# Running sums, row broadcasts and gated scores of the first block's two attentions on fp32r operands, with masks in bf16

## The reference, cut to what matters

```
w[i, j] = exp(z[i, j] - sum over k from j to i-1 of softplus(z[i, k]))     for j < i, else 0
```

```
s[i, j] = (q_i . k_j) * 128**-0.5 * exp(u[j] - m[i])     for j <= i, else 0
h[i]    = sum_j s[i, j] v_j / max(|sum_j s[i, j]|, floor[i])
```

## Time and profile before

| | |
|---|---|
| median of 3 executions | 3308.29 us (3307.25 to 3311.25) |
| the profiled execution's own time | 3307.8 us |
| span of its trace | 3306.0 us |
| busy share of the span | PE 95%, PEld 83%, DVE 61%, ACT 38%, POOL 37% |
| first stick-breaking score matmul | at 242.94 us |
| first gated `ml_decay` | at 353.67 us |
| last numerator and denominator done | at 412.3 us |

### The profile page before, as it was taken

How to read it: one execution, slowest core, us unless ns; L and a number is a source line. 1 busy time by engine, 2 the same in 40 slices (tenths; PEclk the granted TensorE clock), 3 DMA queues, 4 the chain that set the end, 5 groups by cost and what they waited for, 6 DMA issues and landing times.

```text
span 3306.0 us, 49756 instructions
## 1 busy us (share of the span) xinstructions
PE 3147.9 (95%) x18745; PEld 2743.0 (83%) x18745; DVE 2018.0 (61%) x3200; ACT 1255.9 (38%) x2157; POOL 1213.6 (37%) x593
## 2 busy tenths in 40 slices
PE   5989989998899999999998999899999999999998
PEld 2765568998888888888887888699999965799998
DVE  4663440999987788788886255466632554466622
ACT  2334242444983333333333233432222444432221
POOL 1420034467224454454553322144434510244432
PEclk8999899999999999999999999799999999999999
DMA  5630023456569999999995211022223210122221
GB/s 226 227 103 0 0 89 95 131 168 198 187 228 334 334 340 339 337 347 343 349 351 197 64 46 39 20 90 89 89 89 96 91 39 1 39 89 89 89 90 64
DMA packets 181098, 507.16 MB, mean 153 GB/s; under 512 B 15840, under 2 KB 73184, under 8 KB 176736
## 3 DMA queue, kind: packets, MB, share of 16 engines
q1 hardware_dynamic: 72000, 262.18, 24.2%
q0 software_dynamic: 36864, 134.23, 11.0%
q10 hardware_dynamic: 72096, 108.93, 9.9%
HBM read 465.43 MB, written 39.85 MB: 153 GB/s over the span
## 4 chain that ended last, share of the span: by engine, by line
PE 86%; ACT 6%; DVE 5%; issue 2%; DMA 1%; ACTq 0%; DVEq 0%
PE ps L1178 22%; PE ps L1129 16%; PE ps L1066 14%; PE ps L1413 8%; PE ps L842 6%; ACT arena L1787 2%; PE ps L1296 2%; PE ps L1243 2%; PE ps L892 1%; PE ps L937 1%; ACT arena L1803 1%; PE ps L1560 1%; DVE arena L2221 1%; PE ps L1308 1%; PE ps L1196 1%
## 5 line engine op out<-in xcount | busy, mean ns | idle before, releaser
L2141 POOL TENSOR_TENSOR w_lo<-ring,w_hi 128x1024 fp32r<-128x1024 f32 x296 | 749.8, 2537 | 1515.9 <-ACT w_hi L738 1515.5
L738 ACT ACTIVATE w_hi<-ring 128x1024 fp32r<-128x1024 f32 x500 | 525.0, 1055 | 796.9 <-PE ps L1129 272.1
L1129 PE MATMUL ps<-w_hi,arena_r 128*128 128x512 f32 x1536 | 426.7, 397 | 4.7 <-DVE arena_r L2575 4.7
L1066 PE MATMUL ps<-h_hi,w_hi 128*128 128x384 f32 x1024 | 355.9, 348 | 5.3 <-issue 5.3
L1178 PE MATMUL ps<-h_hi,w_hi 128*128 128x264 f32 x1712 | 351.6, 287 | 2.0 <-DVE arena L2672 2.0
L1178 PE MATMUL ps<-h_lo,w_hi 128*128 128x264 f32 x1712 | 350.3, 286 | 0.0
L1178 PE MATMUL ps<-h_hi,w_lo 128*128 128x264 f32 x1712 | 349.8, 286 | 0.0
L1066 PE MATMUL ps<-h_lo,w_hi 128*128 128x384 f32 x1024 | 349.2, 341 | 0.0
L1129 PEld LDWEIGHTS ps<-w_hi,arena_r 128*128 128x128 f32 x1536 | 289.1, 189 | 72.3 <-DVE arena_r L2575 5.5
L1066 PE MATMUL ps<-h_hi,w_lo 128*128 128x384 f32 x1024 | 346.8, 339 | 0.0
L2564 DVE TENSOR_TENSOR w_lo<-ring,w_hi 128x1024 fp32r<-128x1024 f32 x188 | 228.4, 1222 | 134.3 <-ACT w_hi L738 132.8
(11 more groups left out here) (337 smaller groups left out, 5702.1 us busy)
## 6 DMA issues: line engine op xcount, KB each, us to landing
ring<-weight_stream SPq DMA_DIRECT2D x500, 512.0 KB, 3.8
gates<-arena ACTq DMA_DIRECT2D x12, 2048.0 KB, 7.1
arena<-gates ACTq DMA_DIRECT2D x32, 768.0 KB, 14.4
arena<-w_modulation ACTq DMA_DIRECT2D x16, 1024.0 KB, 6.2
early_acts<-arena ACTq DMA_DIRECT2D x64, 192.0 KB, 2.8
arena<-early_acts ACTq DMA_DIRECT2D x32, 384.0 KB, 7.7
arena<-w_modulation ACTq DMA_DIRECT2D x4, 2048.0 KB, 24.3
x<-x_t ACTq DMA_DIRECT2D x1, 2048.0 KB, 11.4
```

Of the source, the lines that this page charges most:

```text
L738: act.activation(w_hi[:, s, :], ring[:, s, :], ACT.Copy).then_inc(hi_ready, 1)
L1066: last = pe.matmul(ps[:, bank, 0:ND], w, v, start=c == 0 and p == 0, stop=c == DC - 1 and p == 2)
L1129: last = pe.matmul(ps[:, Y_BANKS[b][half], :], a[u], w[v][:, half * BANK:(half + 1) * BANK], start=first and p == 0, stop=final and p == 2)
L2141: pool.tensor_tensor(w_lo[:, s, :], ring[:, s, :], w_hi[:, s, :], ALU.subtract)\
```

## The change

- `sb_between`: softplus is cut into `sp_hi` (ACT, Copy to fp32r, `sb_high`) and `sp_lo` (DVE, difference in place of `sp_buf`, `sb_low`); each of the ten matmuls becomes two in fp32r, one on each part, with the constants `tri` and `neg_ones` rounded to fp32r (`sums_r`).
- The masks `hidden` and `late` and their identity are bf16 copies; ACT makes them and `sums_r` once, near the start of the kernel.
- `ml_decay`: the row of maxima is kept as two parts in one tile `m_parts` of 36 rows (high part in rows 0 to 3, low part in rows 32 to 35, rows between zero), broadcast by one fp32r matmul per block.
- `ml_scores`: q and k are cut into parts (`conv_high` on ACT, `conv_low` on DVE, one chunk of 512 columns in each of the turns h = 1 to 7 and two in the last), and each block has three fp32r matmuls in place of one in fp32.
- Semaphores are merged (`gains_ready` into `mod_ready`, `row_min` into `row_step`, `ffn_zero` into `pads_zeroed`); the points at which engines wait for them stay.

```
@@ PE
-                    last = pe.matmul(causal(0, s)[:, 0:P], ident, cst("hidden"), start=False, stop=True)
+                    last = pe.matmul(causal(0, s)[:, 0:P], ident_b, hidden_b, start=False, stop=True)
             def sb_between(h):
-                pe.wait_ge(sp_ready, h + 1)
+                pe.wait_ge(sp_split, h + 1)
                 wait(pe, logw_ready, h)
...
-                        last = pe.matmul(out[:, (j - s) * P:], cst("tri") if j == s else cst("neg_ones"),
-                                         sp_buf[:, h % 2, o:o + SEQ - j * P], start=j == s, stop=j == TB - 1)
+                        for k, part in enumerate((sp_hi, sp_lo)):
+                            last = pe.matmul(out[:, (j - s) * P:], sums_r[:, 0 if j == s else 1, :],
+                                             part[:, h % 2, o:o + SEQ - j * P], start=j == s and k == 0,
+                                             stop=j == TB - 1 and k == 1)
...
-                    pe.matmul(out, cst("pick_head", ML_HEADS * P, 4)[:, h * P:(h + 1) * P],
-                              m_pad[1][:, SEQ + s * P:2 * SEQ], start=True, stop=False)
-                    last = pe.matmul(out[:, 0:P], ident, cst("late"), start=False, stop=True)
+                    pe.matmul(out, pick_r[:, h * P:(h + 1) * P], m_parts[:, s * P:SEQ], start=True, stop=False)
+                    last = pe.matmul(out[:, 0:P], ident_b, late_b, start=False, stop=True)
...
                 wait(pe, wqk_ready, h)
+                pe.wait_ge(conv_step, CONV1 * DC + ML_HEADS + h + 1)
                 for s in range(TB):
-                    last = pe.matmul(causal(0, s), conv[4 + h][:, s * P:(s + 1) * P], conv[h][:, s * P:SEQ],
-                                     start=True, stop=True)
+                    q, k = ((conv_hi[:, c, lo:hi], conv_lo[c][:, lo:hi])
+                            for c, lo, hi in ((h, s * P, SEQ), (ML_HEADS + h, s * P, (s + 1) * P)))
+                    for i, (w, v) in enumerate(three(q, k)):
+                        last = pe.matmul(causal(0, s), w, v, start=i == 0, stop=i == 2)
@@ ACT
+            act.wait_ge(const_in, 16)
+            for dst, src in ((ident_b, ident), (hidden_b, cst("hidden")), (late_b, cst("late")),
+                             (sums_r.rearrange("p a b -> p (a b)"), cst("sums", 2 * P))):
+                act.activation(dst, src, ACT.Copy).then_inc(cast_done, 1)
...
+            def sb_high(h):
+                act.wait_ge(sp_ready, h + 1)
+                wait(act, between_ready, h - 1)
+                act.activation(sp_hi[:, h % 2, :], sp_buf[:, h % 2, :], ACT.Copy).then_inc(sp_high, 1)
+            def conv_high(c):
+                act.wait_ge(max_step, MAX_STEPS + 2)
+                act.activation(conv_hi[:, c, :], conv[c], ACT.Copy).then_inc(conv_silu, 1)
             sb_copy(0)
             sb_log(0)
+            sb_high(0)
             sb_copy(1)
             for h in range(SB_HEADS):
                 if h + 1 < SB_HEADS:
                     sb_log(h + 1)
+                    sb_high(h + 1)
                 if h == 0:
...
+                    act.wait_ge(max_step, MAX_STEPS + 1)
+                    act.activation(m_parts[0:4, :], m_pad[1][:, SEQ:], ACT.Copy).then_inc(row_act, 1)
+                    act.activation(pick_r, cst("pick_head", ML_HEADS * P, 36), ACT.Copy).then_inc(cast_done, 1)
                 sb_weights(h)
                 if h + 2 < SB_HEADS:
                     sb_copy(h + 2)
+                if h:
+                    conv_high(h - 1)
+                if h == SB_HEADS - 1:
+                    conv_high(h)
@@ DVE
+            def sb_low(h):
+                dve.wait_ge(sp_high, h + 1)
+                dve.tensor_tensor(sp_lo[:, h % 2, :], sp_buf[:, h % 2, :], sp_hi[:, h % 2, :], ALU.subtract)\
+                    .then_inc(sp_split, 1)
+            def conv_low(c):
+                dve.wait_ge(conv_silu, DC + c + 1)
+                dve.tensor_tensor(conv_lo[c], conv[c], conv_hi[:, c, :], ALU.subtract).then_inc(conv_step, 1)
             sb_nabs(0)
             sb_softplus(0)
+            sb_low(0)
+            dve.tensor_copy(m_parts, cst("pick_head", ML_HEADS * P, 36)).then_inc(max_step, 1)
...
                     sb_softplus(h + 1)
                 sb_logw(h)
+                if h + 1 < SB_HEADS:
+                    sb_low(h + 1)
+                if h == 0:
+                    dve.wait_ge(row_act, 4)
+                    dve.tensor_tensor(m_parts[32:36, :], m_pad[1][:, SEQ:], m_parts[0:4, :], ALU.subtract)\
+                        .then_inc(max_step, 1)
+                if h:
+                    conv_low(h - 1)
+                if h == SB_HEADS - 1:
+                    conv_low(h)
```

More of the change, by code:

```diff
@@ L101 @@
 NCONST = 0
-for _n, _k in [("ident", P), ("ones", P), ("ones64", P), ("tri", P), ("neg_ones", P), ("iota", P),
+for _n, _k in [("ident", P), ("ones", P), ("ones64", P), ("sums", 2 * P), ("iota", P),
                ("late", P), ("hidden", P), ("pick_head", ML_HEADS * P), ("first_half", P), ("lowest", CHUNK)]:
@@ L121 @@
 LOG_SEQ = 9
-ROW_STEPS = LOG_SEQ + 3
+PADS = 5
+ROW_MINS = 2
+ROW_STEPS = ROW_MINS + LOG_SEQ + 3
 MAX_STEPS = LOG_SEQ + 2
@@ L252, in build @@
         w_buf = view(5120, 2, 1280, of=work_w)
+        sp_lo = place("sp_lo", [P, 2, 1280], F32R, at=at_w + 2560)
+        sb_r = place("sb_r", [P, 3584], F32R, at=at_h)
+        sp_hi = view(0, 2, 1280, of=sb_r)
+        m_parts = view(2560, SEQ, rows=36, of=sb_r)
+        pick_r = view(3072, ML_HEADS * P, rows=36, of=sb_r)
+        cast = place("cast", [P, 3, P], BF16, at=at_arena + 25200)
+        ident_b, hidden_b, late_b = (cast[:, k, :] for k in range(3))
+        sums_r = view(25392, 2, P, dt=F32R)
+        conv_hi = view(16472, DC, SEQ, dt=F32R)
+        conv_lo = [view(23656, SEQ, dt=F32R)] + [view(6208 + c * (SEQ + CONV1 - 1), SEQ, dt=F32R) for c in range(DC - 1)]
         conv = [view(23656, SEQ)] + [conv_in[:, c, 0:SEQ] for c in range(DC - 1)]
@@ L422, in build @@
         sp_ready = sem("sp_ready")
+        sp_high, sp_split = sem("sp_high"), sem("sp_split")
+        cast_done = sem("cast_done")
         between_ready = sem("between_ready")
@@ L496, in build @@
         zeroed = sem("zeroed")
-        ffn_zero = sem("ffn_zero")
         a_taken = sem("a_taken")
@@ L950, in sb_out @@
                 last.then_inc(y_ready, 1)
+            pe.wait_ge(cast_done, 4)
             sb_scores(0)
@@ L980, in _ @@
             pe.wait_ge(logw_ready, SB_HEADS)
-            pe.wait_ge(conv_silu, 8)
+            pe.wait_ge(cast_done, 5)
+            pe.wait_ge(row_act, 4)
+            pe.wait_ge(max_step, MAX_STEPS + 2)
             def ml_decay(h):
@@ L2245, in _ @@
             dve.memset(conv_in[:, :, 0:CONV1 - 1], 0.0).then_inc(pads_zeroed, 1)
-            dve.wait_ge(pads_zeroed, 5)
+            dve.wait_ge(pads_zeroed, PADS)
             dve.wait_ge(gates_taken, 2)
-            dve.tensor_scalar(n_row, f_row, 0.0, 2.0, ALU.min, ALU.mult).then_inc(row_min, 1)
-            dve.wait_ge(row_min, 1)
-            dve.tensor_tensor(e_row, n_row, f_row, ALU.subtract).then_inc(row_min, 1)
+            dve.tensor_scalar(n_row, f_row, 0.0, 2.0, ALU.min, ALU.mult).then_inc(row_step, 1)
+            dve.wait_ge(row_step, 1)
+            dve.tensor_tensor(e_row, n_row, f_row, ALU.subtract).then_inc(row_step, 1)
             def qk_normed(g):
@@ L2273, in _ @@
             modulation(2 * DC, 4 * DC).then_inc(mod_ready, 1)
-            dve.wait_ge(mod_ready, 2)
+            dve.wait_ge(mod_ready, 3)
             modulated_gain(1, "g_norm2")
@@ L2277, in _ @@
             dve.tensor_scalar(f_row, f_row, 0.0, None, ALU.min).then_inc(row_step, 1)
-            dve.wait_ge(row_step, 1)
+            dve.wait_ge(row_step, ROW_MINS + 1)
             dve.tensor_tensor(f_pad[0][:, SEQ:], f_row, e_row, ALU.subtract).then_inc(row_step, 1)
             for k in range(LOG_SEQ):
-                dve.wait_ge(row_step, k + 2)
+                dve.wait_ge(row_step, ROW_MINS + k + 2)
                 src, dst = f_pad[k % 2], f_pad[(k + 1) % 2]
@@ L2383, in _ @@
             dve.wait_ge(out_added, DC)
-            dve.wait_ge(gains_ready, 2)
+            dve.wait_ge(mod_ready, 4)
             split_normed(dve, s_in2, lambda c: xf[:, c, :], lambda c: gains[:, 1, c:c + 1],
@@ L2792, in ffn @@
                 dve.wait_ge(rstd_ready, n.rooted)
-                dve.memset(a_pad[:, :, 0:CONV2 - 1], 0.0).then_inc(ffn_zero, 1)
-                dve.wait_ge(ffn_zero, k + 1)
+                dve.memset(a_pad[:, :, 0:CONV2 - 1], 0.0).then_inc(pads_zeroed, 1)
+                dve.wait_ge(pads_zeroed, PADS + k + 1)
                 def up(i):
@@ L3058 @@
     constant("ones64", (i // 64 == j // 64).astype(f32))
-    constant("tri", -(i >= j).astype(f32))
-    constant("neg_ones", -np.ones((P, P), f32))
+    constant("sums", np.concatenate([-(i >= j).astype(f32), -np.ones((P, P), f32)], 1))
     constant("iota", j.astype(f32))
@@ L3063 @@
```

(3 more changed lines are left out.)

11 lines of the change are left out of this document (5 added, 6 removed).

## The result

The changed kernel took 3284.32 us (median of 5, 3278.32 to 3290.66) beside 3310.09 us for the kernel before (median of 5, 3307.25 to 3322.22): ratio 0.9915, 95% interval 0.989 to 0.9941. The difference of the medians is 25.8 us; the two profiled spans, 3276.5 and 3306.0 us, differ by 29.5.

A forecast was written before the change was run, and what follows sets the result against it. PE, busy 95% of the span, was taken as the bound until ACT and DVE bind. Terms saved 37.4 us, less 7 for the clock, net 30.4: 3307.8 - 30.4 = 3277.4 us, range 3263 to 3297.

The forecast's parts named there:

- the clock: Allowance for PE running below 2.4 GHz: 7 us, 4 in stick-breaking heads and 3 in gated ones, bounds 0 and 19.
- fill: From 242.94 us to the first head's running sums: 22.7 us against 24.62 before, saving 1.9.
- six turns: Stick-breaking turns, 267.56 to 341.83 us: 10.8 us each, 64.8 against 74.3, saving 9.5.
- start of the gated heads: From 353.67 to 380.67 us: 13.9 us against 27.0 before, saving 13.1.
- Prices: PE step times: 128-column fp32r matmul 0.21 us, bf16 mask 0.15 instead of 0.42; running sums 3.56 against 4.53.
- Half the missing share is lost time: Reading of PEclk before the change: about 9 us lost in stick-breaking heads, about 10 us in gated heads.
- loop of ACT and DVE: In stick-breaking turns, the hand-offs between ACT and DVE take 10.4 us, level with PE's 10.43.
- The forecast's own sign of being wrong: A stick-breaking turn of over 12 us, or any stage after 412 us longer than before.
- rival 3: PE's clock falls in the stick-breaking turns, slower than before: 3323 us at 0.7 throughout, gated heads included; chance 0.04.
- Decay: Gated heads: 36-row fp32r matmul per block and four masks take 1.34 us against 4.50.
- Scores: Gated heads: scores in three passes take 2.2 us against 2.16, no gain, bounds 1.8 and 2.8.
- At no cost: Four casts at the start, under 1.5 us on ACT, and three 0.6 us operations at h = 0 hide in waits.

The follow-up runs named there:

- zero rows: Changed kernel with its four floor-row broadcasts as fp32 matmuls of 128 rows, 124 of them zeros: ratio 0.9898, span 3269.5 us.
- fillers: Changed kernel with 128-row zero-padded broadcasts plus matmuls nobody reads where TensorE waits: ratio 0.9886, span 3267.3 us; with 4-row broadcasts instead, ratio 0.9908.
- the gated heads alone: Kernel before with only decay by parts and gated scores in three passes; masks and running sums as before: ratio 0.9948, span 3289.9 us.
- sums alone: Kernel before with only the running sums in two fp32r passes; masks, decay and gated scores as before: ratio 0.9968, span 3294.6 us.
- masks alone: Kernel before with only the masks in bf16; running sums, decay rows and gated scores as before: ratio 0.9933, span 3290.9 us.
- the last version: Changed kernel with 128-row zero-padded broadcasts, nine unread matmuls ahead of the last running sums, conv_low moved behind the next nabs: median 3272.22 us, ratio 0.9876.
- the full rows: Changed kernel with its four 4-row broadcasts replaced by fp32 matmuls of 128 rows of other data: ratio 0.9892, span 3274.9 us.
- 36 rows and the late take: Changed kernel with floor broadcasts by parts in 36 rows and sb_take moved on DVE behind the low part: ratio 0.9908, span 3278.5 us.

## Why the prediction was right, and where it was not

The forecast of 3277 us in 3263 to 3297 held: 3284.32 measured, and for the profiled execution 29.5 us less span against 30.4 forecast. The sum at full clock was right: the terms without the clock are 131.9 us, and the same stages, measured with the clock held wherever a run shows that, are 132.4. Over these the changed kernel lost 8.0 us to the clock, where 7.0 had been set aside. The size was near and the places were wrong, so that the two agree is luck:

| stretch | forecast, full clock | measured | at full clock in an experiment |
|---|---|---|---|
| fill | 22.7 | 22.2 | not seen (22.2 taken) |
| six turns | 64.8 | 70.3 | 63.8 (zero rows) |
| end | 8.8 | 10.1 | 8.6 (fillers) |
| start of the gated heads | 13.9 | 15.1 | 15.1 (it had 1.00) |
| rest of them | 21.7 | 22.7 | 22.7 (it had 1.00) |
| the clock | 7.0 | in the rows above | |
| sum | 138.9 | 140.4 | 132.4 |

- **Prices.** The mask was right (0.16, forecast 0.15). The 128-column fp32r matmul was mis-sized: 0.21 forecast, 0.06 to 0.12 measured. So running sums are 2.92 us and not 3.56. It hardly mattered in the turns, since ACT and DVE bound them at full clock. The Trainium skill's weight load ("TensorE: Matmul & The Clock Gate", LDWEIGHTS) gives 0.11 us for 128 columns. The trace agrees with it: the loads start 0.11 us apart, and only a matmul behind a wider one steps less. With 0.11 in place of 0.21 the prediction's sum for the running sums would be 2.76 us, an estimate from that page; decays and scores of the four gated heads together would be 1.6 us less, so the 3 us that the prediction puts nearly all there are too much.
- **Sums that don't come out.** The terms printed for the fill add up to 22.1 us and not 22.7, those for the start of the gated heads to 14.1 and not 13.9. "Half the missing share is lost time" is misworded: at PEclk 0.50 a broadcast took 2.02 us instead of 1.12, about twice its time, so the whole missing share (0.08 and 0.17) is lost, and the 9 and 10 us of the prediction are worked out that way. None of these moves the forecast by more than 0.6 us.
- **The turn.** The step that a loop of ACT and DVE of 10.4 to 10.5 us would come up level with PE was right: 10.60 us with the clock at 1.00. But it was covered: in the changed kernel removing two links of it moved nothing.
- **The clock** was the step that failed in its place. Forecast were 4 us in the stick-breaking heads and 3 in the gated ones. Measured against the kernel with zero rows it cost 6.4 us in the turns, against the fillers 1.5 at the end, and none in the gated heads, which ran at 1.00. The forecast's own sign of being wrong came true: turns of over 12 us with PEclk under 0.85 is what it names for rival 3. PEclk was 0.83 there, and the turns of h = 2 to 4 were 12.2 to 12.6 us against the 12.48 of a turn at full clock before. For the whole to be slower, rival 3 needed the gated heads to run near 1.2 GHz too, and they went the other way. Wherever their decays went by parts, the gated stretches together had 0.92 to 1.00 (0.92 in the gated heads alone, also 1.00 with their scores back in fp32); wherever by matmuls of 4 rows, 0.83 to 0.87 (before, sums alone, masks alone).
- **Decay** was mis-sized: 1.34 forecast, 1.89 measured; matmuls of 36 rows step 0.43 us at 512 columns, 0.2 us more than 128 rows do; 4 rows in fp32 had stepped 1.05 and I didn't carry such an excess over. Scores came out cheaper (1.94, forecast 2.2), so that a round was 8.27 instead of 7.9.
- **At no cost** held: the fill was no longer than forecast with the operations of m_parts in it, and the first score matmul stood at 242.45 us, before at 242.94. That PE's idle time ahead of the last running sums would grow from 3.7 to 5.0 us (329.9 to 334.9) was not foreseen, where the prediction had gaps mostly under 1 us; the last head's path through ACT and DVE has no scores of another head to cover it, and PE's own work in that turn fell from 6.8 to 5.6 us while the turn stayed as long (10.47 and 10.58 us).

The Trainium skill's rule on idle gaps ("TensorE: Matmul & The Clock Gate", HAM oscillation), that they put PE back to half clock, was weighed with rival 3. The runs agree with it where PE stood idle for 5 us: 334.90 to 345.02 us at 0.83, and 1.00 when fillers covered the gap. They show more than it says: the clock fell with PE without idle time, and held with a microsecond idle in every turn.

## What to carry to other kernels

When matmuls get shorter, look at PEclk of each stretch again before counting the gain: here masks and sums that shrank by 2.6 us a turn gave nothing in three turns of six, in two of them because the clock fell. A small broadcast may be cheaper with all 128 rows than with 4, even where 124 of them hold zeros: the six turns went from 70.3 to 63.8 us, and the broadcast itself steps 0.81 to 0.91 us (zero rows, 276.18 us with fillers and 294.87 us in the last version) instead of 1.05. It costs one memset. And once PE is no longer the bound, the order in which DVE and ACT hand small side jobs to each other ahead of the next head is worth as much as a matmul: one moved instruction gave 1.1 us in two of six turns and 0.2 to 0.3 in three.

## What was not expected of the hardware

- Of the kernels with bf16 masks and fp32r sums, four whose broadcasts had 128 rows had PEclk of 0.94 to 1.00 over the six turns; six with 4 or 36 rows had 0.80 to 0.90. With PE busy the clock fell once in the turns of one of the four and not in those of the others, and three or four times in each of the six. Zeros in the added rows did no worse than values.
- Two fp32r matmuls of 128 columns behind a wider one step 0.06 and 0.11 us. At 1.2 GHz such a pair steps 0.11 + 0.21 (from 257.97 us in the changed kernel).
- The fill of kernels with bf16 masks and fp32r sums and without fillers was 22.2 to 22.5 us in six profiles and 26.3 and 26.2 in two (with the full rows, whose fill has the changed kernel's instructions, and with 36 rows and the late take), with PEclk about 0.69 and 0.55: when the clock comes back seems to hang on more than the instructions. This stays open.
